# A-head attention: the next pair's score matmuls put directly behind the values of the pair one back, in TensorE's queue

## What is computed

```python
h = rmsnorm(x, pre_g)
p = jnp.einsum('btd,de->bte', h, w_in)
aq, ak, av, ag, bq, bk, bv, bg = split_projection(p)
# A: 8 heads over 2 K/V heads, chunks of 64 tokens, window of 2 chunks, a learned sink per head
s = jnp.einsum('bcqkgd,bcskd->bckgqs', qb, kb) * scale
s = jnp.where(valid[None], s + bias[None], NEG_INF)
p = jax.nn.softmax(jnp.concatenate([s, sink], axis=-1), axis=-1)[..., :-1]
o = jnp.einsum('bckgqs,bcskd->bcqkgd', p.astype(v.dtype), vb)
ya = o.reshape(bsz, t, A_WIDTH) * jax.nn.silu(ag)
# B: 4 heads, two softmax maps per head, in blocks of 128 queries
attn = p[:, :, 0] - lam * p[:, :, 1]
yb = rmsnorm(o, subln_g) * (1.0 - lambda_init) * jax.nn.silu(bg)
y = jnp.einsum('bte,ed->btd', jnp.concatenate([ya, yb], axis=-1), w_out)
x = x + rmsnorm(y, post_g)
```

## Time and profile before

| | us |
|---|---|
| median of 3 runs | 515.28 (515.09 to 517.2) |
| the profiled execution, its own time | 516.69 |
| its span | 514.9 |
| TensorE busy | 502.5 (98%) |
| VectorE busy | 283.8 (55%) |
| ScalarE busy | 260.0 (50%) |
| GpSimd busy | 105.3 (20%) |

### The profile page before, as it was taken

One profiled execution on the slowest core, in us unless ns is written; L12 is line 12 of the kernel. 1 busy time (PEld: TensorE's weight loads), 2 busy tenths in 40 slices (PEclk: granted clock), 3 DMA queues, 4 the chain that ended last, 5 costly groups with the idle time before them and its releaser, 6 DMA issues.

```text
span 514.9 us, 7476 instructions
## 1 busy us (share of the span) xinstructions
PE 502.5 (98%) x2724; PEld 422.0 (82%) x2724; DVE 283.8 (55%) x676; ACT 260.0 (50%) x622; POOL 105.3 (20%) x139
## 2 busy tenths in 40 slices
PE   8999999999999999999999999999999999999995
PEld 8999987888877888888887777688788888888884
DVE  4959734555557545545457687554663593433332
ACT  7932543556575557656577766633644471222211
POOL 1070503223032021213043335212303000000000
PEclk9999999999999999999999999999999999999998
DMA  8810042020111010110002010111000834322221
GB/s 313 266 46 0 2 121 81 12 71 0 42 43 24 19 41 1 42 41 17 26 1 74 10 42 0 43 43 41 1 0 1 193 136 148 126 95 83 81 92 72
DMA packets 41540, 32.05 MB, mean 62 GB/s; under 512 B 18784, under 2 KB 36128, under 8 KB 41504
## 3 DMA queue, kind: packets, MB, share of 16 engines
q1 hardware_dynamic: 38912, 26.85, 18.2%
q10 hardware_dynamic: 2592, 4.72, 2.5%
HBM read 26.88 MB, written 4.19 MB: 60 GB/s over the span
## 4 chain that ended last, share of the span: by engine, by line
PE 85%; DVE 5%; ACT 4%; issue 3%; DMA 2%; POOL 1%; SPq 0%; DVEq 0%; POOLq 0%; ACTq 0%
PE proj L1212 39%; PE scores L1318 15%; PE scores L1143 8%; PE scores L1233 6%; PE banks L1254 6%; PE banks L1244 3%; PE scores L1279 2%; DVE k_stack L993 2%; PE proj L1143 1%; PE banks L1143 1%; PE banks L1299 1%; PE banks L1287 1%; DMA w_raw<-in_w_in 1%; DVE a_weights L1079 1%; ACT weights L801 1%
## 5 line engine op out<-in xcount | busy, mean ns | idle before, releaser
L645 POOL TENSOR_TENSOR w_lo<-w_raw,w_hi 128x256 fp32r<-128x256 f32 x84 | 62.9, 779 | 170.4 <-ACT w_hi L726 170.4
L1212 PE MATMUL proj<-hT_hi,w_hi 128*128 128x512 f32 x336 | 89.9, 400 | 1.4 <-DVE q_stack L988 0.8
L1212 PE MATMUL proj<-hT_hi,w_lo 128*128 128x512 f32 x336 | 89.5, 401 | 0.0
L1212 PE MATMUL proj<-hT_lo,w_hi 128*128 128x512 f32 x336 | 88.5, 400 | 0.0
L1048 DVE CUSTOM_DVE_ANT_0 weights<-scores,dist_b 128x128 f32<-128x128 f32 (+7 forms) x64 | 45.9, 754 | 53.9 <-PE scores L1233 53.7
L1212 PEld LDWEIGHTS proj<-hT_hi,w_hi 128*128 128x128 f32 x336 | 60.6, 188 | 14.6 <-DVE q_stack L988 1.2
L1212 PEld LDWEIGHTS proj<-hT_hi,w_lo 128*128 128x128 f32 x336 | 60.6, 188 | 13.3 <-issue 1.9
L1212 PEld LDWEIGHTS proj<-hT_lo,w_hi 128*128 128x128 f32 x336 | 60.6, 188 | 11.9 <-issue 0.8
L801 ACT ACTIVATE weights<-weights,small 128x128 f32<-128x128 f32 (+7 forms) x64 | 49.0, 767 | 15.1 <-DVE small L1048 15.1
L811 ACT ACTIVATE weightsT<-banks 128x512 f32<-128x512 f32 (+3 forms) x48 | 23.6, 491 | 56.1 <-PE banks L1244 56.0
L1233 PE MATMUL scores<-k_stack,q_stack 128*128 128x512 f32 (+3 forms) x192 | 41.8, 353 | 0.0
(11 more groups left out here) (125 smaller groups left out, 749.3 us busy)
## 6 DMA issues: line engine op xcount, KB each, us to landing
w_raw<-in_w_in SPq DMA_DIRECT2D x13, 512.0 KB, 3.8
w_raw<-in_w_in SPq DMA_DIRECT2D x16, 256.0 KB, 3.7
x_res<-in_x SPq DMA_DIRECT2D x8, 512.0 KB, 4.4
out<-y_out ACTq DMA_DIRECT2D x16, 256.0 KB, 2.3
x_all<-in_xT SPq DMA_DIRECT2D x7, 512.0 KB, 7.1
wo_raw<-in_w_out SPq DMA_DIRECT2D x8, 256.0 KB, 5.3
wo_raw<-in_w_out SPq DMA_DIRECT2D x4, 512.0 KB, 9.1
wv_raw<-in_w_in SPq DMA_DIRECT2D x8, 160.0 KB, 6.6
```

The costliest lines, as they stand in the source:

```text
L645: nc.gpsimd.tensor_tensor(w_lo[:, n % SPLIT, k], w_raw[:, n % RAW, k], w_hi[:, n % SPLIT, k].bitcast(F32), ALU.subtract).then_inc(w_lo_rea ...
L1212: last = nc.tensor.matmul(to, w[:, slot, k, :], h[:, k, HALF * half:HALF * half + HALF], start=(p == 0 and k == first), stop=(p == PIECES ...
```

## The change

The step of the scores of pair p+2 (and, ahead of it, the step a_weights of chunk 2(p+1)+1, which belongs to VectorE) is put into the list directly behind the values of pair p. Where it stood before it is left out.

```diff
@@ -157,7 +157,7 @@
-        if last[0] == "a":
+        if last[0] == "a" and ("a_weights", 2 * last[1] + 1) not in steps:
             steps.append(("a_weights", 2 * last[1] + 1))
...
@@ -165,7 +165,7 @@
-        elif kind == "a":
+        elif kind == "a" and ("a_scores", now) not in steps:
             first.append(("a_scores", now))
...
@@ -205,6 +205,8 @@
             steps.append((f"{which}_values", unit))
+            if which == "a" and kind == "a" and now + 1 < STEPS_A:
+                steps += [("a_weights", 2 * now + 1), ("a_scores", now + 1)]
             if which == "b" and unit % 4 == 3:
```

## The result

| | before | changed |
|---|---|---|
| median | 516.34 us (6 runs, 515.09 to 517.20) | 519.09 us (6 runs, 518.90 to 519.89) |
| ratio | | 1.0064, 95% interval 1.0049 to 1.0079 |
| span of the profiled execution | 514.9 us | 517.7 us |

The kernel became slower by 0.64%, clearly; the two medians differ by 2.75 us. The forecast was 518.0 us, with a chance of only one half for slower. The median of the kernel before is 1.1 us higher here than the 515.28 that the forecast stood on: of its six runs two took 515.09 and 515.28 us and four 516.09 to 517.20, and the three known at the forecast held both of the low ones. By its interval the ratio is 2.5 to 4.1 us, and the sum of +2.68 us lies in it.

A forecast was written before the change was run, and what follows sets the result against it. TensorE, busy 502.5 of 514.9 us, was taken to bound the kernel. Changes in the A heads' pairs 1 to 6 summed to +2.68 us, for a forecast of 518.0 us, range 516.4 to 519.6.

The forecast's parts named there:

- the sum of +2.68 us: A heads, pairs 1 to 6: changes in TensorE's stretches to the values, +0.70, +0.87, +1.19, -0.55, +0.63, -0.16 us.
- How the numbers follow: Whole kernel: slower by over 0.5% 0.50, within it 0.45, faster 0.05; range 516.4 to 519.6 us.
- The ends +1.7 and +3.6: A heads: the sum is 1.0 us smaller or larger, by the price of going from values to scores.
- the one price that was in no row: TensorE, A heads: going from values directly to scores, taken as the 0.39 us that projection loads wait there.
- rivals that ended at no change or faster: A heads: ScalarE's copy not in the way, 512.2 us, 5%; change of shape worth more, 515.6 us, 10%.
- the signal from ScalarE to TensorE: A heads: 0.06 us allowed for the signal after ScalarE's copy, set in ten places.
- The other signs: A heads profile: TensorE's waits on the transposes' copy rise to 4 to 6 us, GpSimd waits go, VectorE waits less.
- the four distances: A heads, TensorE: from piece to values 5.6, 5.7, 6.7 and 4.7 us in pairs 1 to 4.
- First: A heads: scores come some 3.2 us earlier, so first transposes stop waiting for GpSimd's scaling; 0.39 us in pair 3.
- Second: TensorE, A heads: the change from transposes to scores goes; transposes to a piece take 0.39 us, to scores 0.58.
- Third: A heads: scores covered ScalarE's copy; one piece leaves 1.31 us, the copy needs 1.37, much more with ScalarE busy.
- The other side: A heads: ScalarE's copy is not in the way of the second transposes; -3.05 us, 512.2 us, 5%.

The follow-up runs named there:

- moved_late: Only the scores of pairs 5, 6 and 7 moved, the rest as in the kernel before: 1.0003 of the kernel before.
- before_bank_copies_first: Kernel before, with second transposes in their own bank and both ScalarE copies ahead of the exponentials, scores in their old place: 0.9988 of the kernel before.
- bank_copies_first: Changed kernel, with second transposes in their own bank and both ScalarE copies ahead of the exponentials: 513.44 us, 0.9933 of the kernel before.
- piece_between: Changed kernel, with one projection piece put between the values and the moved scores: 1.0083 of the kernel before.

## Why the prediction came out as it did

**Where it failed** is the step "How the numbers follow", which comes behind the sum. The waits that the sum names are there, and its +2.68 us stand against +2.70 in the table below. That step put the sum on too low a level and set it against too coarse a threshold. So it gave 0.45 to no difference that can be told, although the sum was slower at both of its ends.

- The level: 515.28, the median of three runs. The six runs of the comparison have 516.34, 1.06 us more, and that is nearly all of the 1.09 us between 518.0 and 519.09.
- "A measurement of this kernel can tell about 0.5%, 2.58 us, from no change." With six runs each the interval is 0.15% to either side, some 0.8 us. A sum of 2.68 us is then a measurable slowdown, not a toss-up at a threshold.
- The ends +1.7 and +3.6, from the one price that was in no row. The loads of the scores waited 0.38 to 0.39 us at each of the six places, as the projection's loads had there (in the row of the scores' loads, two of some 0.17 and six of 0.38 or 0.39 make the 2.6 us). The middle was the right value, and even the lower end was a slowdown. The Trainium skill (TensorEngine Tiling (Array Packing), section Tiling Modes, Key Properties) has the array drain at each change of tiling mode. That the loads wait at all six places agrees with it; how long, it does not say.
- 15% for rivals that ended at no change or faster. In the earlier trace rows the second transposes already came late with scores and a piece as their cover, and without a cover the copy could only be waited for longer.

**The terms of the sum**, from the stretches of the changed kernel (from the piece, in pairs 5 and 6 from the first transposes, to the values, in us; the change is with 1.19 for the scores and against before):

| pair | predicted | measured | change predicted | change measured |
|---|---|---|---|---|
| 1 | 5.57 | 5.67 | +0.70 | +0.80 |
| 2 | 5.72 | 5.79 | +0.87 | +0.94 |
| 3 | 6.75 | 6.75 | +1.19 | +1.19 |
| 4 | 4.69 | 4.76 | -0.55 | -0.48 |
| 5 | 4.56 | 4.40 | +0.63 | +0.47 |
| 6 | 4.38 | 4.32 | -0.16 | -0.22 |
| sum | | | +2.68 | +2.70 |

(The A heads grew by 2.63; the 0.07 is in what follows the values.) **That the sums agree to 0.02 us is luck in part**: pairs 1, 2 and 4 came out 0.24 us dearer than predicted, pairs 5 and 6 0.22 cheaper. The mis-sized term is the signal from ScalarE to TensorE. Ahead of second transposes it took 0.14 to 0.15 us, not 0.06: in pair 2 the copy ends at 289.36, the transposes begin at 289.50. The rows that I had showed it: 296.55 + 0.60 to 297.29 is 0.14. The 0.06 holds ahead of the values only. In pair 5 the exponentials started 0.1 us sooner behind the rounding than I had them, and its values waited 0.49 us where I had named 0.8 as a sign. The other signs came as named: 4.6 us of waits on the copies (4 to 6), no wait for GpSimd, and the four distances.

- **First** (no more waits for GpSimd): right; moved_late shows a second cause for it that I had missed, the 1.19 us of the next pair's scores that now stand ahead of the first transposes.
- **Second** (a change of shape saved): right, 0.2 us in each of six pairs, shown by before_bank_copies_first against bank_copies_first and by piece_between.
- **Third** (the cover over ScalarE's copy decides): right, shown from both sides: with the bank and the order of the copies, with pieces as cover, and by taking the rounding out from ahead of the copy.
- **The other side** (512.2 us, if the copy were not in the way): its mechanism was sound and its price right. bank_copies_first is that case made true: 2.90 us less in the A heads for the 3.05 worked out. It took two edits that the change did not have.

## What to carry to other kernels

Work that stands between two steps on a busy engine may be hiding another engine's queue: before moving it, write down when the thing behind it can start at the earliest, from the other engine's rows, and what is ahead of that in its queue. If two waits stand one behind the other, each fix alone shows little (1.13 and 1.03 us here) and both together show all (5.53); cost them as a chain. And when a sum keeps its sign at both ends of its one uncertain price, let the chance follow the sum, and take what a measurement can tell from the scatter and number of its runs.

## What the runs showed of the hardware that I had not expected

- Going from values to scores directly costs the weight loads 0.39 us, as much as from values to a projection piece, while scores behind transposes cost 0.17. From a projection piece to scores it is 0.37. In these rows it goes by what the array was last doing, not by what comes next. The loads of the scores behind transposes and behind values in the changed kernel, and behind a piece in piece_between:

```profile
267.05 1.07 PEld L1281 LDWEIGHTS scores<-kT_A,qT_A 64*128 64x128 f32 x16 [0.17 <-issue]
...
272.67 1.07 PEld L1281 LDWEIGHTS scores<-kT_A,qT_A 64*128 64x128 f32 x16 [0.39 <-issue]
```

```profile
292.49 1.07 PEld L1284 LDWEIGHTS scores<-kT_A,qT_A 64*128 64x128 f32 x16 [0.37 <-issue]
```

- The A heads start some 2 us earlier in some profiled executions (264.3 to 264.7 us in five kernels) than in others (266.0 to 266.8 in six, 265.5 in one), though nothing ahead of them differs between the kernels. Between the kernel before and piece_between the difference arises in the first 11 us, where at first the same matmuls take nearly twice as long. TensorE in the kernel before:

```profile
7.70 1.27 PE L1143 MATMUL scores<-wv_hi,hT_lo 128*128 128x320 f32 x4
8.76 0.73 PE L1143 MATMUL proj<-wv_hi,hT_lo 128*128 128x320 f32 x2
...
10.66 0.75 PE L1143 MATMUL scores<-wv_hi,hT_hi 128*128 128x320 f32 x4
11.25 0.46 PE L1143 MATMUL proj<-wv_hi,hT_hi 128*128 128x320 f32 x2
```

and in piece_between, up to the same matmuls:

```profile
6.70 0.75 PE L1148 MATMUL scores<-wv_hi,hT_lo 128*128 128x320 f32 x4
7.29 0.46 PE L1148 MATMUL proj<-wv_hi,hT_lo 128*128 128x320 f32 x2
...
8.75 0.85 PE L1148 MATMUL scores<-wv_hi,hT_hi 128*128 128x320 f32 x4
```

From start to start the first four take 1.06 us and 0.59. In the kernel before, too, such a group takes 0.59 from 10.66 us on; by then it is 1.91 us behind, and at the A heads 1.80. The granted clock of the stretch reads 1.00 in both; what makes the difference is open, and no run here was made for it. Because spans of single executions differ by 2 us in this way between kernels whose A heads are alike, I compared the A heads.
